# Layer-2 mixers: attention output turned by the products themselves, division moved to ScalarE, scores and wide products in another order

## The reference, cut to what matters

```
proj = rmsnorm(x) @ w_in
att = sliding-window attention with sinks   # 4 heads of 64, window of 128 tokens + own chunk
ssd = state-space mixer                     # 8 heads of 64, chunked
gdn = gated delta net                       # 4 heads of 64, a triangular solve in each 64-token chunk
mix = concat(att, ssd, gdn) @ w_out         # (256 + 512 + 256) columns by 1024
x = x + rmsnorm(mix)
```

## Time and profile before

| | |
|---|---|
| median of 3 runs | 2243.07 us |
| profiled execution, its own time | 2243.37 us |
| its span | 2241.6 us |
| TensorE busy over the span | 2205.8 us, 98% |
| VectorE, ScalarE, GpSimd busy | 71%, 41%, 12% |
| mixers of layer 2 | about 1280 to 1604 us of the span |
| one steady step (n = 3 to 7) | about 35.2 us |

### The profile page before, as it was taken

How to read it: one execution, slowest core, us unless ns; L and a number is a source line. 1 busy time by engine, 2 the same in 40 slices (tenths; PEclk the granted TensorE clock), 3 DMA queues, 4 the chain that set the end, 5 groups by cost and what they waited for, 6 DMA issues and landing times. The chain is left out here.

```text
span 2241.6 us, 34318 instructions
## 1 busy us (share of the span) xinstructions
PE 2205.8 (98%) x13067; PEld 1815.9 (81%) x13067; DVE 1584.9 (71%) x2212; ACT 915.4 (41%) x1672; POOL 262.2 (12%) x266
## 2 busy tenths in 40 slices
PE   8999999999999999999999989999999999999997
PEld 7888888888888888887888777887888888888886
DVE  5657668876665546657698798887797777765557
ACT  5443544343333321234344454555433233334444
POOL 0222232100000000001222242322020000000000
PEclk9999999999999999999999999999999999999999
DMA  4111111134333264433232452323234434448655
GB/s 154 48 38 57 38 48 48 67 132 160 122 113 112 94 244 179 155 118 120 98 113 100 151 172 66 114 86 114 103 128 187 160 155 164 159 164 298 213 183 183
DMA packets 106952, 289.06 MB, mean 129 GB/s; under 512 B 9692, under 2 KB 35388, under 8 KB 102332
## 3 DMA queue, kind: packets, MB, share of 16 engines
q1 hardware_dynamic: 106812, 287.14, 36.5%
HBM read 205.01 MB, written 82.10 MB: 128 GB/s over the span
## 5 line engine op out<-in xcount | busy, mean ns | idle before, releaser
L124 PE MATMUL psG<-h_hi,w_hi 128*128 128x512 f32 (+1 forms) x624 | 164.2, 395 | 0.4 <-PEq L4310 0.3
L124 PE MATMUL psG<-h_hi,w_lo 128*128 128x512 f32 (+1 forms) x624 | 161.6, 391 | 0.0
L124 PE MATMUL psG<-h_lo,w_hi 128*128 128x512 f32 (+1 forms) x624 | 161.4, 392 | 0.0
L455 POOL TENSOR_TENSOR sb_w<-sb_left 128x128 f32<-128x128 f32 (+3 forms) x96 | 97.0, 1015 | 320.0 <-DVE sb_left L582 320.0
L124 PEld LDWEIGHTS psG<-h_hi,w_lo 128*128 128x128 f32 x624 | 111.4, 188 | 20.2 <-DVE w_lo L155 0.2
L124 PEld LDWEIGHTS psG<-h_hi,w_hi 128*128 128x128 f32 x624 | 110.1, 188 | 21.6 <-issue 2.5
L124 PEld LDWEIGHTS psG<-h_lo,w_hi 128*128 128x128 f32 x624 | 111.1, 188 | 20.1 <-issue 0.5
L582 DVE TENSOR_TENSOR_SCAN sb_left<-sb_left 128x128 f32<-128x128 f32 (+3 forms) x96 | 102.7, 1077 | 2.1 <-ACT sb_left L468 1.4
L155 DVE TENSOR_TENSOR w_lo<-w_raw,w_hi 128x1024 fp32r<-128x1024 f32 x48 | 58.6, 1223 | 55.1 <-ACT w_hi L150 55.1
L150 ACT CAST w_hi<-w_raw 128x1024 fp32r<-128x1024 f32 x48 | 50.3, 1049 | 115.1 <-PE psG L124 62.0
L2028 POOL TENSOR_TENSOR features_T<-m_bias_both 128x512 f32<-128x512 f32 x10 | 15.7, 1569 | 676.6 <-DMA m_bias_both<-in_proj_pairs 631.3
(11 more groups left out here) (659 smaller groups left out, 5935.1 us busy)
## 6 DMA issues: line engine op xcount, KB each, us to landing
w_raw<-in_units SPq DMA_DIRECT2D x76, 512.0 KB, 4.3
w_raw<-hidden_blocks SPq DMA_DIRECT2D x77, 256.0 KB, 2.9
merge_gates<-features_T SPq DMA_DIRECT2D x12, 1024.0 KB, 7.5
merge_gates<-merge_gates SPq DMA_DIRECT2D x12, 1024.0 KB, 4.9
features<-features_T SPq DMA_DIRECT2D x24, 512.0 KB, 2.6
w_spare<-in_units SPq DMA_DIRECT2D x22, 512.0 KB, 4.4
down_sums<-w_spare SPq DMA_DIRECT2D x22, 512.0 KB, 3.3
hidden_blocks<-features_T SPq DMA_DIRECT2D x11, 1024.0 KB, 3.9
```

The costliest lines, as they stand in the source:

```text
L124: return pe.matmul(out, lhs, rhs, start=first, stop=last, skip_group_check=True)
L455: pool.tensor_tensor(w, left_chunk(S, 1), left_chunk(S), ALU.subtract).then_inc(w_ready, 1)
```

## The change

The scores are divided before they are turned: `den` and `rden` move ahead of `nc0` on VectorE, and ScalarE multiplies each head's 256 exponentials by the inverse (`n0` to `n3`). The transposes of the scores move on TensorE from behind X32 to behind X64. In the attention product the operands change places: the values are stationary (64 columns), the turned scores move (128 columns), and the result has features on partitions, heads 0 and 3 in one bank and 2 and 1 in another, in both halves of the partitions; the rows of `w_out` are laid out to match. The product is made in one piece after `wt`, and `yo` comes behind it. ScalarE rounds the result (`ah`), VectorE takes the remainder (`att`), so `mtrm` turns four blocks instead of six, and `mtm` and `mlo` work on 512 columns instead of 768. The state-space scores (`sc`) come before T8, and the attention's scores are made in one piece before X8. The four wide products of `x32` move to `t64`. Step n = 2 gets 14 more products that nobody reads, 256 columns wide (`THIRD`).

```diff
-        A6_HI, A6_LO = ([room.take(f"a_{n}{s}", [P, 6, P], F32R) for s in range(2)] for n in ("hi", "lo"))
-        RAW, X, GP, M = (room.take(n, [P, D]) for n in ("raw", "x", "gpost", "mix"))
+        A4_HI, A4_LO = ([room.take(f"a_{n}{s}", [P, 4, P], F32R) for s in range(2)] for n in ("hi", "lo"))
+        RAW, X, GP = (room.take(n, [P, D]) for n in ("raw", "x", "gpost"))
+        M = room.take("mix", [P, 768])
+        A0_HI, A0_LO = ([room.take(f"a0_{n}{s}", [P, 2, P], F32R) for s in range(3 if n == "hi" else 2)] for n in ("hi", "lo"))
...
-        scalF = Steps(sem("scalar_front"), "qk sq vb z ga lnr expr xs kt e0 e1 e2 e3 es pt")
+        scalF = Steps(sem("scalar_front"), "qk sq vb z ga lnr expr xs kt e0 e1 e2 e3 es n0 n1 n2 n3 pt ah")
         scalG = Steps(sem("scalar_chain"), "T2 yq0 yq1 yln yexp T4 mtm T8 T16 T32 vu0 vu1 va vo1 vo0 T64 wt vn osq oln oexp")
-        vectF = Steps(sem("vector_front"), "ss ssc nqk kb qg swab mx mx2 ngm sdif dsub dmask nc0 nc1 nc2 nc3 nt qkd sd0 sd1 den rden "
+        vectF = Steps(sem("vector_front"), "ss ssc nqk kb qg swab mx mx2 ngm sdif dsub dmask den rden nc0 nc1 nc2 nc3 nt qkd sd0 sd1 "
                                            "yo yx att st1 y yz st2")
...
-                    scalG.done("mtm", a.copy(A6_HI[i % 2][:], bank(3, 2)[:, 0:6 * P].rearrange("p (c t) -> p c t", c=6)))
+                    scalG.done("mtm", a.copy(A4_HI[i % 2][:], bank(3).rearrange("p (c t) -> p c t", c=4)))
...
+                def divided(h):
+                    scalF.wait(a, f"e{h}", n)
+                    scalF.done(f"n{h}", a.activation(SS[:, h], SS[:, h], ACT.Copy, scale=rden[:, h:h + 1]))
+
+                if n == 0:
+                    decayed()
+                if chain and not front:
+                    high(1)
                 if front:
+                    vectF.wait(a, "rden", n)
+                    divided(0)
+                if chain:
+                    product(64)
+                if front:
+                    divided(1)
+                    if prod is not None:
+                        root(prod)
+                    divided(2)
+                    divided(3)
                     tensF.wait(a, "ptr", n)
                     tensF.wait_last(a, "att", n)
                     scalF.done("pt", a.copy(PTR[:].rearrange("p n t -> p (n t)"), bank(1, 2)))
-                    if n == 0:
-                        decayed()
-                elif chain:
-                    high(1)
-                if chain:
-                    product(64)
-                if front and prod is not None:
-                    root(prod)
+                def attended():
+                    tensF.wait(a, "att", n)
+                    if n >= 3:
+                        tensA.wait(a, "a6", n - 3)
+                    scalF.done("ah", a.copy(A0_HI[n % 3][:], PS[:, 1:3, 0:P]))
...
+                if front and not chain:
+                    attended()
...
+                    if front:
+                        attended()
...
-                    vectG.done("mlo", tt(A6_LO[i % 2][:], bank(3, 2)[:, 0:6 * P].rearrange("p (c t) -> p c t", c=6), A6_HI[i % 2][:].bitcast(F32), ALU.subtract))
+                    vectG.done("mlo", tt(A4_LO[i % 2][:], bank(3).rearrange("p (c t) -> p c t", c=4), A4_HI[i % 2][:].bitcast(F32), ALU.subtract))
...
+                    scalF.wait(v, "es", n)
+                    vectF.done("den", tt(den[:], sums[:], es[:], ALU.add))
+                    vectF.wait(v, "den", n)
+                    vectF.done("rden", v.reciprocal(rden[:], den[:]))
...
-                    tensF.wait(v, "att", n)
-                    tensG.wait_last(v, "mtrm", n)
-                    vectF.wait(v, "rden", n)
-                    vectF.done("att", tt(heads(M[:, 0:256], AH), heads(PS[:, 1, 0:256], AH), per(rden[:], AH, 64), ALU.mult))
+                    scalF.wait(v, "ah", n)
+                    vectF.done("att", tt(A0_LO[n % 3][:], PS[:, 1:3, 0:P], A0_HI[n % 3][:].bitcast(F32), ALU.subtract))
...
+                        for _ in range(THIRD.get(at, 0)):
+                            weights_pass(pe, PS[:, 0, 256:512], w_hi[0][:, 0:P], w_hi[1][:, 0:256], True, True)
...
-                def attention(first):
-                    for h in (first, first + 1):
-                        kv = 64 * (h // 2)
-                        mm(PS[:, 1, 64 * h:64 * h + 64], PTR[:, 2 * h], VP[:, kv:kv + 64], True, False)
-                        x = mm(PS[:, 1, 64 * h:64 * h + 64], PTR[:, 2 * h + 1], GA[:, 256 + kv:320 + kv], False, True)
+                def attention():
+                    for pair in ((0, 1), (2, 3)):
+                        for m in range(2):
+                            for h in pair:
+                                kv = 64 * (h // 2)
+                                values = GA[:, 256 + kv:320 + kv] if m else VP[:, kv:kv + 64]
+                                x = mm(PS[half(h), 2 if h in (1, 2) else 1, 0:P], values, PTR[:, 2 * h + m], m == 0, m == 1)
                     return x
...
-                    turn(tensG, "mtrm", 3, [M[:, c * P:(c + 1) * P] for c in range(6)])
-                level_t(8)
-                if n == 0:
-                    pe.wait_ge(c_here, 16)
-                    unread(2)
+                    turn(tensG, "mtrm", 3, [M[:, c * P:(c + 1) * P] for c in range(4)])
                 if front:
 
                     poolF.wait(pe, "keep0", n)
@@ -3199,6 +3223,11 @@
                     for g in range(2):
                         x = mm(PS[:, 0, g * P:(g + 1) * P], BC[:, g], BC[:, 2 + g])
                     tensF.done("sc", x)
...
                     scores((0, 2))
+                    tensF.done("swas", scores((1, 3)))
                 level_x(8)
-                if front:
-                    tensF.done("swas", scores((1, 3)))
                 fill("t16")
...
-                if front:
-                    for h in range(AH):
-                        if h % 2 == 0:
-                            scalF.wait(pe, f"e{h + 1}", n)
-                        for m in range(2):
-                            x = pe.transpose(PS[:, 1 + h // 2, (2 * (h % 2) + m) * P:(2 * (h % 2) + m + 1) * P], SS[:, h, m * P:(m + 1) * P], C["ident"][:])
-                    tensF.done("ptr", x)
...
                 if front:
+                    for h in range(AH):
+                        scalF.wait(pe, f"n{h}", n)
+                        for m in range(2):
+                            x = pe.transpose(PS[:, 1 + h // 2, (2 * (h % 2) + m) * P:(2 * (h % 2) + m + 1) * P], SS[:, h, m * P:(m + 1) * P], C["ident"][:])
+                    tensF.done("ptr", x)
+                if chain and not front:
+                    turn_h(2)
+                fill("wt")
+                if chain:
+
+                    vectG.wait(pe, "VT64", i)
+                    poolG.wait(pe, "kbg", i)
+                    for h in range(GH):
+                        x = mm(PS[half(h), 5, (h // 2) * P:(h // 2) * P + P], KBG[:, 64 * h:64 * h + 64], VT[:, h])
+                    tensG.done("wt", x)
+                if front:
                     scalF.wait(pe, "pt", n)
                     scalF.wait(pe, "ga", n)
                     poolF.wait_last(pe, "vprev", n)
-                    attention(0)
-                    if n == 0:
-                        tensF.done("att", attention(2))
-                        unread(3)
+                    tensF.done("att", attention())
+                if n == 0:
+                    unread(3)
+                if front:
                     vectF.wait(pe, "qkd", n)
                     vectF.wait_last(pe, "st2", n)
                     for g in range(2):
                         x = mm(PS[:, 4, 256 * g:256 * g + 256], BC[:, 2 + g], ST[:, 256 * g:256 * g + 256])
                     tensY.done("yo", x)
-                if chain and not front:
-                    turn_h(2)
-                fill("wt")
-                if chain:
-
-                    vectG.wait(pe, "VT64", i)
-                    poolG.wait(pe, "kbg", i)
-                    for h in range(GH):
-                        x = mm(PS[half(h), 5, (h // 2) * P:(h // 2) * P + P], KBG[:, 64 * h:64 * h + 64], VT[:, h])
-                    tensG.done("wt", x)
-                if front and n:
-                    tensF.done("att", attention(2))
...
+THIRD = {"x16": 6, "t32": 2, "x32": 6}
 OWN = ("x2", "t4", "x4", "t16")
-FILL = {"x2": (32, 34), "t4": (34, 38), "x4": (38, 42), "t16": (42, 48), "x16": (0, 3), "t32": (3, 7), "x32": (7, 11), "t64": (11, 15),
+FILL = {"x2": (32, 34), "t4": (34, 38), "x4": (38, 42), "t16": (42, 48), "x16": (0, 3), "t32": (3, 7), "x32": (7, 7), "t64": (7, 15),
         "x64": (15, 18), "wt": (18, 24), "vn": (24, 24), "o": (24, 24), "end": (24, 32)}
-FILL_FIRST = {"x2": (0, 2), "t4": (2, 6), "x4": (6, 10), "t16": (10, 16), "x16": (16, 17), "t32": (17, 18), "x32": (18, 19), "t64": (19, 21),
```

(32 more changed lines are left out.)

24 lines of the change are left out of this document (9 added, 15 removed).

## The result

The changed kernel is slightly slower. Its median is 2248.67 us (15 runs, 2246.36 to 2250.51) against 2244.24 us (15 runs, 2241.86 to 2248.89), a ratio of 1.0016 with a 95% interval of 1.0009 to 1.0023. The forecast was 2242.0 us and the range 2235.5 to 2247.5; the time lies outside it. The medians differ by +4.4 us where -1.1 was forecast. The profiled execution has a span of 2246.9 us, 5.3 more than the one before.

What follows compares the result with a forecast made beforehand. TensorE's own list and its waits were taken to bound the five steady steps, other engines n = 0 to 2. Terms 0.2 + 0 - 1.5 + 0.6 - 0.4 = -1.1 us gave 2242.0 us, range 2235.5 to 2247.5.

Steps and rivals of the forecast that it cites:

- First step: Step n = 0: TensorE up to 3.3 us late but VectorE busy well after; +0.2 us, bounds -0.7 and +1.0.
- T8 and X8: Moved scores on TensorE: `sc` ahead gives ScalarE time for `mtm`, X8's copy is long done; no cost.
- The rule on the clock: Steady steps: frequent short TensorE idles make the clock swing; new waits of 0.4 and about 1.0 us taken as nearer n = 1.
- +4.1 for `pt`: First step: the turned copy starts about 4.1 us later, behind `L` (1.5), four divisions (1.3) and their wait for `rden`.
- Two new waits, steady step: TensorE waits for `va` before T64 (0.4 us) and for divisions behind `root`; net +0.12 a step, +0.6 over five.
- n = 1: Step n = 1: VectorE is full, smaller `mlo` and moved denominator operations about cancel; 0, bounds -0.3 and +0.3.
- n = 8: Step n = 8: the chain through `mtm` shortens, a third fewer columns and two transposes less; -0.4 us, bounds 0 and -0.5.
- n = 2: Step n = 2: unread products fill most of the wait before T32, the clock holds, VectorE sets the end; -1.5 us.
- A: Steady steps: the new waits do not arise; five times -1.23, -6.1 us instead of +0.6, 2235.3; chance 0.10, part of it 0.08.
- C: Attention product: the halves do not overlap; 0.84 us more in each of six steps, +5.0, 2247.1; chance 0.07.
- D: Step n = 2: the clock falls as before; +1.5 to 2.0 us on the forecast, 2243.5 to 2244; chance 0.16.
- B: Steady steps: new idles drop the clock; +2.3 us a step, +11.5 in five, 2253.5; chance 0.05.

Runs made afterwards that it cites:

- e2: Kernel before, with only `sc` moved ahead of T8 and of the first step's two unread products: 2246.58 us against 2243.57 before, ratio 1.0009.
- e3: Changed kernel with `root` on ScalarE behind all four divisions: 2245.30 us against 2243.57 before, ratio 1.0004.
- e1: Changed kernel with the first step's two unread products ahead of `sc` again: 2247.64 us against 2243.57 before, ratio 1.0014.
- e5: Changed kernel, first step: two unread products ahead of `sc`, ten instead of three before score transposes, none before `yo`: 2245.03 us against 2243.91 before, ratio 0.9999.
- e6: Changed kernel without the first step's three unread products ahead of `yo`: 2247.26 us against 2243.91 before, ratio 1.0013.
- e7: Changed kernel with ten unread products instead of three ahead of the first step's score transposes: 2247.04 us against 2243.91 before, ratio 1.0011.
- e10: Changed kernel with the edits of e8 and e9 together: 2241.14 us against 2244.96 before, ratio 0.9977.
- e4: Changed kernel without the 14 unread products in step n = 2: 2249.46 us against 2243.57 before, ratio 1.0024.
- e9: Changed kernel with SyncE's four 512 KB loads in n = 7 held until the queries are turned: 2247.50 us against 2244.96 before, ratio 1.0010.
- e8: Changed kernel with e5's and e3's edits, VT64 earlier on VectorE, two wide products moved from `wt` to `t64`: 2243.07 us against 2243.91 before, ratio 0.9992.

## Why the prediction was wrong, by its own steps

**The step that failed** is "First step": "I take +0.2, bounds -0.7 and +1.0". It measured +5.5. Its reasoning had three holes, each visible in the rows:

1. It rested on VectorE being "itself busy till well after" and did not read by how much. Before, `yo` on TensorE ended at 1296.58 and VectorE came to it at 1298.81: a cover of 2.2 us. After, VectorE reached the same place at 1300.61 (1305.55 less 4.94), which counted from the start of the mixers is 0.84 later than before; `yo`'s product was 7.7 us later. A lateness of 7.7 with a cover of 2.2 and 0.84 cannot be hidden: VectorE came 0.84 later and then waited 4.94, and 5.53 of these 5.8 are still there at V2. Even the forecast's own 3.3 was 1.1 beyond the cover.
2. The moved `sc` was priced at nothing for T8 and X8. In n = 0 it also moved ahead of two unread products that stood in a wait. e2 prices that at 0.85 us with the clock held, and the changed kernel shows 2.46 with the clock down.
3. The rule on the clock was weighed for the steady steps, where the idles are 0.47 and 0.65, and not for the first step, where "+4.1 us" for `pt` meant an idle of several microseconds ahead of the transposes. The Trainium skill (TensorE: Matmul & The Clock Gate, A second HAM failure mode) says that frequent short idles between groups of matmuls make the clock swing. The trace of the changed kernel agrees in the first step, where the idles are 1.95, 3.40 and 1.10 us, and does not where they are 0.47 and 0.65 with full work between; behind the same 1.95 us the clock held in e2 and e3. The evidence from n = 1 was weak too: behind the same 0.95 us the clock fell in e1.

The forecast's +4.1 for `pt` was near for what it counted. `pt` starts 7.07 us later (18.92 us after the start of the mixers against 11.85), of which 2.46 came in with the scaling; the other 4.6 are `L`, the divisions and their wait, and the transposes, which are 1.75 us long between the divisions. Then the attention gave back nothing, because it ran at half rate: `pt` to `yo` is 0.64 longer where 0.84 less was expected. e5 undoes most of this inside n = 0 and removes the slowdown, so this step is the cause of most of the +5.3 span (its three edits were not told apart beyond e1, e6 and e7, and each of these met a fall of the clock elsewhere). Of the 0.2% by which the medians differ, the single parts (e1, e6, e7) are too small for their intervals; their traces tell them apart, and e5 and e10 are clear against the changed kernel by their intervals.

**Two new waits, steady step**: right, mechanism and place, each start to 0.1 us. The net of a step was forecast at +0.12 and measured -0.13 in most of them: before, a step takes 35.18, after 35.05. The stalls came out at 0.47 and 1.05 (1.90 for the transposes less 0.85), where I had 0.4 and about 1.0. The divisions are slower than priced (0.49 to 0.51 us each and 0.40 apart, against 0.42 and 0.33), but the end of the transposes is only 0.08 off. What was mis-sized is the rest of the step, from `vn` to the next X16, which gives back 0.6 us and not 0.30: the two transposes fewer 0.31, and the scores and `sc` in one run 0.29. The attention was 0.98 against 1.04. e3 shows that `root` is what the second wait hangs on, and that the wait behind it, VT64, takes 0.34 back.

**n = 1** 0.0 and **n = 8** -0.48 against 0 and -0.4: right. **n = 2** -1.63 against -1.5: right, and the mechanism too: the wait of 0.49 us before `wt` is for VectorE's VT64, which the forecast named as the end. There are still waits of 0.95 us before qk, 0.71 and 0.43, and the clock held. In e4, without THIRD, the step took 37.04. That it held is in part luck: in e6 and e7 it fell in this step with THIRD in place.

**Not in the sum**: the gap of 1.05 us in n = 7, which I had no row for. Nothing in the change adds a load there. It goes in e9 when the loads are put off, but it is missing in e5 and e7 with them as well, so its cause stays open. The changed kernel's execution happened to have it: about 1 of the 5.3 us.

**Rivals.** A did not come: both waits arose, and `root` waited 0.68 us for VectorE. C did not: the halves overlap. D did not in this execution. B was wrong in its place: the clock held in n = 3 to 7 of the changed kernel, and fell behind idle time in the first step, for which I had no rival.

**Left open.** The start of the mixers moves by up to 2.8 us between executions (1278.55 before, 1279.51 after, 1281.36 in e10). What makes the clock fall in one execution and hold in another of the same code is open, and so are all gaps without a releaser in T16, and the waits of 1.65 to 2.08 us for VectorE in n = 6 of e5, e8 and e10.

## What to carry to other kernels

When a piece is said to be hidden, read the slack at the place where its result is taken (end of the product against the start of its reader) and subtract; in a filling step the engine that sets the pace can change. An order written for the steady step must be priced again in the first step, above all where filler work stood in a wait that a moved piece now passes. In the product of the turned scores and the values, which had only 64 moving columns, exchanging the operands paid here (16 passes in 0.98 us instead of 1.88); the Trainium skill (TensorEngine Tiling (Array Packing), When to Use Tiling) names that swap for a moving side of 64 or less, and the trace agrees. And when the same code meets a different clock from one execution to the next, one trace of each version is not enough to price a part of 1 or 2 us.

## What the runs showed of the hardware that I had not expected

- The granted clock is not a function of the code alone. e5 and e8 have the same first step, with waits of 0.4 us before the transposes and 1.10 before the attention in both; in e5 the clock went to 0.55, in e8 it held at 1.00, and V2 came at 27.56 and 25.07: 2.5 us. In e2 and e3 `sc` waits as long as in the changed kernel (1.95 us, 0.59 behind it there), and the clock held. In n = 1 the waits of 0.45 and 0.95 us stand in the changed kernel, e1, e5, e7 and e8; in e1 alone the clock fell behind them.
- With three products taken out, the clock stayed down longer: e6, 0.50 until after 1308, against 0.79 at 1304 to 1306 in the changed kernel. One execution each; that the one caused the other is not shown.
- TensorE can stand still for 1.0 to 1.6 us in the middle of a group of small products with nothing that it waits for in the profile (after, e1, e3, e7, e8). Behind the one of 1.60 us the clock fell to 0.50. In the changed kernel 2 MB of loads kept the DMA engines about 90% busy at that time; with them put off (e9, e10) the gap of n = 7 was not there, and neither was it in e5 and e7 with them.
